# First stage of a two-layer decoder trunk: DMA order x, gate, x, up, and 256-column products for units 0 and 1

## The chip, the cores and the metric

The kernel runs on one core of one Trainium2 chip. The metric is the device time of one execution in microseconds (us), median of three runs. Besides these there is one profiled execution, from which all rows below come.

## The reference, cut to what matters

A trunk of two layers on a sequence of 256 tokens with 1024 channels, all float32. Each layer is SwiGLU, mixer, SwiGLU, each followed by a layer norm of `alpha*x + sub`; layer 0 mixes by causal pooling, layer 1 by sliding-window attention.

```python
def swiglu(x, w_gate, w_up, w_down):
    h = jax.nn.silu(x @ w_gate) * (x @ w_up)
    return h @ w_down
...
x = post_norm(x, 0.5 * swiglu(x, ffn_w_gate[i, 0], ...), ln_g[i, 0], ln_b[i, 0])
```

There are four SwiGLUs, each with gate and up matrices of 1024 x 2816 and a down matrix of 2816 x 1024. Only the first one's start is touched by the change.

## The kernel before, in words

The hidden width of 2816 is cut into 22 **units** of 128. For each unit TensorE (PE) makes gate and up products into PSUM (8 blocks of 128 input channels each), ScalarE (ACT) takes silu of the gate, VectorE (DVE) multiplies by up, and PE multiplies the result with the down weights into four accumulators (`ffn_down`). To reach float32 accuracy at speed, weights and activations are split into a high and a low part of type fp32r, and three fp32r products stand for one (`three`, L1056 to L1059). ACT makes the high part (L459 for gate and up, L467 for down), DVE the low part (L720, L724).

The first two units of every SwiGLU are not split: `gate_up_raw` (L1061) multiplies plain float32 weights `raw_g` with the channel-major activations `xf`, in two halves `t` of 128 tokens. The trace records each such float32 product as two matmuls, so that 8 channel blocks give 16 records. `xf` comes from `transposes(e, t)` (L1114, matmuls of L1123: 8 blocks of `xn`), whose first bank DVE copies (L797) and whose second ACT copies (L496). The order at the start of PE (L1132 to L1138), for the first SwiGLU, is: transposes of half 0; unit 0 half 0, gate and up; unit 1 half 0, gate; transposes of half 1; unit 1 half 0, up; unit 0 half 1; unit 1 half 1. Then come two small transposes of layer norm parameters (L1144), `ffn_down(0, 0)`, `gate_up(0, 2)` from split weights, `ffn_down(0, 1)` and so on.

The loads of the start are issued by SyncE's queue (SPq, L262 to L270) in this order: x half 0, gate unit 0, up unit 0, x half 1, gate unit 1, up unit 1 (512 KB each), down unit 0 (512 KB), gate and up of units 2 and 3 (1024 KB each), down unit 1 in two pieces, down units 2 and 3. The gate and up of unit 0 have semaphores of their own (`unit0_in[0]`, `unit0_in[1]`), those of unit 1 share `g_in[0]`, which has to reach 32. The load of units 4 and 5 overwrites the buffer of units 0 and 1 and waits for `g_used` = 2 (L238), which PE raises once per finished unit. Small loads, the identity matrix among them, are issued by ACT's queue.

ACT and DVE work through their instructions in program order: copies of both halves of `xf`, high and low parts of x (L510, L806), split of down unit 0, then per unit silu, high part of h, and for unit 0 also the split of unit 2's gate and up, then the split of the next down weights. `gate_up(0, 2)` waits for the low parts of unit 2 (`g_lo_done`, L1081).

Of the kernel before, what the change touches and what calls it, by code (L numbers as in the profile page):

```python
# [21 lines left out]
P = 128  # L22
D = 1024
S = 256
F = 2816
KT = D // P
TT = S // P
# [39 lines left out]
def trunk_kernel(nc, x, positions, ln_g, ln_b, w_gate, w_up, w_down, pool_w, pool_b, pool_scale,  # L67
# [8 lines left out]
    with ExitStack() as ctx:  # L76
# [21 lines left out]
        xf = sb("xf", [P, TT, KT, P])  # L98
# [28 lines left out]
        ps = ctx.enter_context(nc.psum_tensor("ps", [P, 8, 512], f32))  # L127
        ACC = [[ps[:, 2 * t + h, :] for h in range(2)] for t in range(TT)]
        WORK = 4

        g_in = [sem("g_in0"), sem("g_in1")]
        unit0_in = [sem("unit0_gate_in"), sem("unit0_up_in"), sem("unit0_down_in")]
# [69 lines left out]
        def raw_unit(G, half):  # L202

            c = raw_g[:, (G // 2) % 2, half, :].rearrange("p (k f) -> p k f", k=KT)
            return c[:, :, (G % 2) * P:(G % 2 + 1) * P]
# [18 lines left out]
        @block.sync  # L224
        def _(sp):
            gate_v = w_gate.rearrange("l i (k p) f -> (l i) p k f", p=P)
            up_v = w_up.rearrange("l i (k p) f -> (l i) p k f", p=P)
            down_v = w_down.rearrange("l i (u p) d -> (l i) p u d", p=P)
            qkv_v = w_qkv[0].rearrange("(k p) c -> p k c", p=P)
            wo_v = w_o[0].rearrange("(u p) d -> p u d", p=P)  # L230
            pool_v = pool_w[0].rearrange("g (k p) d -> p k g d", p=P)

            def load_gate_up(f, c, it=0):

                C = G0[f] // 2 + c

                if c == 2:
                    sp.wait_ge(g_used, G0[f] + RAW_UNITS)  # L238
                elif c > 2:
                    sp.wait_ge(g_lo_done, 2 * (X0[f] + 2 * c - 2) + 8 * it)  # L240
                elif f > 0:
                    sp.wait_ge(g_lo_done, 2 * (X0[f] + 2 * c))
                dst = raw_g[:, C % 2, :, :].rearrange("p m (k f) -> p m k f", k=KT)
                for m, w in enumerate((gate_v, up_v)):
                    sp.dma_start(dst[:, m], w[f, :, :, bass.ds(2 * P * c + 4 * P * it, 2 * P)]).then_inc(g_in[C % 2], 16)

            def load_down(f, c, it=0):

                E = D0[f] // 2 + c
                after(sp, d_lo_done, 2 * (E - 1) + 4 * it)  # L250
                for m in range(2):
                    sp.dma_start(raw_d[:, E % 2, m, :], down_v[f, :, bass.ds(2 * c + m + 4 * it, 1), :].rearrange("p a d -> p (a d)")).then_inc(d_in[E % 2], 16)

            def load_d(E, srcs):
                after(sp, d_lo_done, 2 * (E - 1))
                for m, src in enumerate(srcs):
                    dst = raw_d[:, E % 2, m, :]
                    sp.dma_start(dst.rearrange("p (g d) -> p g d", g=4) if len(src.shape) == 3 else dst, src).then_inc(d_in[E % 2], 16)


            first = raw_g[:, 0, :, :].rearrange("p m (k f) -> p m k f", k=KT)
            for t in range(TT):  # L262
                sp.dma_start(xn[:, t, :], x[0, t * P:(t + 1) * P, :]).then_inc(x_in[t], 16)
                for m, w in enumerate((gate_v, up_v)):
                    sp.dma_start(first[:, m, :, t * P:(t + 1) * P], w[0, :, :, t * P:(t + 1) * P]).then_inc(unit0_in[m] if t == 0 else g_in[0], 16)
            sp.dma_start(raw_d[:, 0, 0, :], down_v[0, :, 0, :]).then_inc(unit0_in[2], 16)
            load_gate_up(0, 1)
            for h in range(2):
                sp.dma_start(raw_d[:, 0, 1, 512 * h:512 * (h + 1)], down_v[0, :, 1, 512 * h:512 * (h + 1)]).then_inc(d_in[0], 16)
            load_down(0, 1)  # L270
            for f in range(FFNS):
                for c in range(2 if f == 0 else 0, 3):
                    load_gate_up(f, c)
                    load_down(f, c)
                with sp.Fori(0, (UNITS // 2 - 3) // 2) as it:
                    for c in range(3, 5):
                        load_gate_up(f, c, it)
                        load_down(f, c, it)
                if f == 0:
                    load_d(D_POOL // 2, [pool_v[:, k] for k in range(2)])  # L280
                if f == 2:

                    for i, j in enumerate((2, 0, 1)):
                        C = G_QKV // 2 + i
                        sp.wait_ge(g_lo_done, 2 * (X_QKV - 2 + 2 * i))
                        for m in range(2):
                            sp.dma_start(raw_g[:, C % 2, m, :].rearrange("p (k c) -> p k c", k=4),
                                         qkv_v[:, 4 * m:4 * m + 4, 512 * j:512 * (j + 1)]).then_inc(g_in[C % 2], 16)
                        if i < 2:
                            load_d(D_WO // 2 + i, [wo_v[:, 2 * i + m] for m in range(2)])  # L290
                    for i in range(2, 4):
                        load_d(D_WO // 2 + i, [wo_v[:, 2 * i + m] for m in range(2)])
            for t in range(TT):
                for h in range(2):
                    sp.wait_ge(y_done, 2 * t + h + 1)
                    sp.dma_start(out[0, t * P:(t + 1) * P, 512 * h:512 * (h + 1)], xn[:, t, 512 * h:512 * (h + 1)]).then_inc(out_done, 16)
            sp.wait_ge(out_done, 64)
# [755 lines left out]
        def _(pe):  # L1053
# [7 lines left out]
            def gate_up_raw(f, u, t, ms=(0, 1)):  # L1061

                e, G = FFN_EVENT[f], G0[f] + u
                if f > 0 and u == 0 and t == 0 or f == 0 and u == 1 and t == 0 and ms[0] == 0:
                    pe.wait_ge(g_in[(G // 2) % 2], 32 * (G // 4 + 1))
                for m in ms:
                    if f == 0 and u == 0 and t == 0:
                        pe.wait_ge(unit0_in[m], 16)

                    for i, k in enumerate((0, 4, 1, 5, 2, 6, 3, 7) if f > 0 else range(KT)):  # L1070
                        if m == 0 and u == 0:
                            pe.wait_ge((xf_lo_done, xf_up_done)[k // 4], 8 * e + 4 * t + k % 4 + 1)
                        last = pe.matmul(ps[:, WORK + u % 2, m * S + t * P:m * S + (t + 1) * P], raw_unit(G, m)[:, k, :],  # L1073
                                         xf[:, t, k, :], start=i == 0, stop=i == KT - 1)
                if t == TT - 1:
                    last.then_inc(g_used, 1)

            def gate_up(f, u, it=0):
# [50 lines left out]
            for f in range(FFNS):  # L1129
                e = FFN_EVENT[f]  # L1130

                transposes(e, 0, used=(0, 2, 1, 1)[f])  # L1132
                gate_up_raw(f, 0, 0)
                gate_up_raw(f, 1, 0, (0,))
                transposes(e, 1)
                gate_up_raw(f, 1, 0, (1,))
                gate_up_raw(f, 0, 1)
                gate_up_raw(f, 1, 1)  # L1138
                if f == 0:

                    pe.wait_ge(small_in, 64)
                    pe.wait_ge(xf_up_done, 8)
                    for a in range(2):
                        last = pe.transpose(ps[:, 7, 48 * a:48 * (a + 1)], lnrow[:, a, :], ident[0:48, 0:48])  # L1144
                    last.then_inc(lnT_ps, 1)
                ffn_down(f, 0)
                with pe.Fori(0, (UNITS - 6) // 4) as it:
                    for u in range(2, 6):
                        gate_up(f, u, it)
                        ffn_down(f, u - 1, it=it)  # L1150
                last_u = UNITS - 4
                gate_up(f, last_u)
                ffn_down(f, last_u - 1)
                gate_up(f, last_u + 1)
                ffn_down(f, last_u, (0,))
                gate_up(f, last_u + 2)
                ffn_down(f, last_u + 1, (0,))
                gate_up(f, last_u + 3)
                ffn_down(f, last_u + 2, (0,))
                ffn_down(f, last_u, (1,))  # L1160
                ffn_down(f, last_u + 3, (0,))
                ffn_down(f, last_u + 1, (1,))
                ffn_down(f, last_u + 2, (1,))
                if f != 2:
                    ffn_down(f, last_u + 3, (1,))
                if f == 0:
                    pool_pe(pe, three)
                if f == 2:
                    attention_pe(pe, three, down, transposes, lambda: ffn_down(2, UNITS - 1, (1,)))
# [39 lines left out]
```

## Time and profile before

| what | us |
|---|---|
| median of 3 runs | 919.07 |
| the three runs | 919.07, 917.87, 919.52 |
| span of the profiled execution, first to last instruction | 916.1 |
| PE busy in it | 875.6 (96%) |
| first raw float32 product starts | 7.09 |
| last raw float32 product of units 0 and 1 ended, parameter transposes start | 27.96 |
| last PE work of the span ends, about | 906 |

The page of the profile gives no device time for the profiled execution apart from its span; the median of the runs lies 2.97 us above the span. Times in rows are microseconds from the start of the span. A matmul's duration (275 ns and the like) contains its latency; successive matmuls overlap, so what counts for the time is the distance between their starts.

### The profile page before, as it was taken

The numbers are of one execution on the slowest core, as the hardware profiler recorded it, in microseconds if no ns is written. First come the engines' busy times: TensorE is split into PE (matmuls) and PEld (weight loads), VectorE is DVE, ScalarE is ACT, GpSimd is POOL, SyncE is SP. The second block draws the span as 40 slices with busy tenths as digits, with TensorE's granted clock in tenths as the row PEclk, the third lists the DMA queues.
The fourth block names the chain that finished last, engine by engine and source line by source line (L and its number), as shares of the span: only waits on it lengthen the run. The fifth ranks groups of instructions, "written<-read, shape, count | busy, mean of one in ns | idle before, by whom it ended". The sixth has DMA issues, their size and how long they took to land.

```text
span 916.1 us, 14933 instructions
## 1 busy us (share of the span) xinstructions
PE 875.6 (96%) x5954; PEld 805.0 (88%) x5954; DVE 540.4 (59%) x758; ACT 380.1 (41%) x622; POOL 76.3 (8%) x71
## 2 busy tenths in 40 slices
PE   6999999997999999999999999988999999999995
PEld 6999999986999999998999999976766899999994
DVE  1764455488674455447665545568687775445445
ACT  2444344322444344333434433435575434434430
POOL 0020000066100000001040000023000100000001
PEclk9999999999999999999999999999999999999998
DMA  9886546254485555660865565450127096555501
GB/s 293 304 289 219 183 160 207 97 176 141 170 301 184 197 172 181 211 202 2 275 239 184 173 217 175 161 218 15 42 101 254 20 311 234 183 189 177 184 1 46
DMA packets 116275, 162.30 MB, mean 177 GB/s; under 512 B 3968, under 2 KB 97760, under 8 KB 116240
## 3 DMA queue, kind: packets, MB, share of 16 engines
q1 hardware_dynamic: 112656, 152.06, 49.2%
q0 software_dynamic: 2496, 9.44, 2.8%
q8 instruction: 24, 0.39, 0.2%
q10 hardware_dynamic: 1088, 0.32, 0.1%
q14 instruction: 11, 0.09, 0.0%
HBM read 160.75 MB, written 1.05 MB: 177 GB/s over the span
## 4 chain that ended last, share of the span: by engine, by line
PE 82%; DVE 10%; ACT 3%; POOL 2%; issue 1%; DMA 1%; SPq 0%; POOLq 0%; DVEq 0%; ACTq 0%
PE ps L1057 25%; PE ps L1058 25%; PE ps L1059 25%; PE ps L1073 5%; DVE stats L759 2%; DVE xn L758 2%; DMA raw_g<-in_ffn_w_up 1%; POOL rstd L356 1%; DVE xn L774 1%; PE ps L1123 1%; PE ps L943 1%; ACT silu L403 1%; PE ps L934 1%; PE ps L937 1%; POOL rstd L358 1%
## 5 line engine op out<-in xcount | busy, mean ns | idle before, releaser
L1059 PE MATMUL ps<-xT_hi,g_lo 128*128 128x256 f32 x1280 | 362.2, 283 | 0.0
L1058 PE MATMUL ps<-xT_lo,g_hi 128*128 128x256 f32 x1280 | 362.2, 283 | 0.0
L1057 PE MATMUL ps<-xT_hi,g_hi 128*128 128x256 f32 x1280 | 361.8, 283 | 0.0
L1057 PEld LDWEIGHTS ps<-xT_hi,g_hi 128*128 128x128 f32 x1280 | 245.4, 192 | 3.2
L1058 PEld LDWEIGHTS ps<-xT_lo,g_hi 128*128 128x128 f32 x1280 | 245.4, 192 | 3.1
L1059 PEld LDWEIGHTS ps<-xT_hi,g_lo 128*128 128x128 f32 x1280 | 245.4, 192 | 0.0
L720 DVE TENSOR_TENSOR g_lo<-raw_g,g_hi 128x1024 fp32r<-128x1024 f32 x171 | 206.5, 1247 | 42.0 <-ACT g_hi L459 41.9
L471 ACT ACTIVATE silu<-ps 128x256 f32<-128x256 f32 x88 | 33.8, 384 | 393.0 <-PE ps L1059 386.1
L728 DVE TENSOR_TENSOR hf<-silu,ps 128x256 f32<-128x256 f32 x88 | 37.0, 421 | 263.0 <-ACT silu L471 263.0
L459 ACT ACTIVATE g_hi<-raw_g 128x1024 fp32r<-128x1024 f32 x172 | 172.0, 1052 | 4.9 <-PE ps L943 4.4
L1057 PE MATMUL ps<-d_hi,hT_hi 128*128 128x512 f32 x352 | 138.7, 394 | 2.0 <-DVE hT_lo L733 2.0
L1058 PE MATMUL ps<-d_lo,hT_hi 128*128 128x512 f32 x352 | 137.9, 392 | 0.0
L1059 PE MATMUL ps<-d_hi,hT_lo 128*128 128x512 f32 x352 | 137.0, 389 | 0.0
L724 DVE TENSOR_TENSOR d_lo<-raw_d,d_hi 128x1024 fp32r<-128x1024 f32 x98 | 122.8, 1254 | 2.6 <-ACT d_hi L467 2.6
L467 ACT ACTIVATE d_hi<-raw_d 128x1024 fp32r<-128x1024 f32 x98 | 102.7, 1049 | 3.1 <-PE ps L1059 3.0
L1059 PEld LDWEIGHTS ps<-d_hi,hT_lo 128*128 128x128 f32 x352 | 66.1, 188 | 14.5
L1057 PEld LDWEIGHTS ps<-d_hi,hT_hi 128*128 128x128 f32 x352 | 66.4, 189 | 14.0 <-DVE hT_lo L733 2.4
L1058 PEld LDWEIGHTS ps<-d_lo,hT_hi 128*128 128x128 f32 x352 | 66.4, 189 | 10.6
L1073 PE MATMUL ps<-xf,raw_g 128*128 128x128 f32 x512 | 61.7, 282 | 3.8 <-DMA raw_g<-in_ffn_w_up 3.2
L1073 PEld LDWEIGHTS ps<-xf,raw_g 128*128 128x128 f32 x512 | 60.1, 197 | 5.4 <-DMA raw_g<-in_ffn_w_up 3.4
L733 DVE TENSOR_TENSOR hT_lo<-hf,hT_hi 128x256 fp32r<-128x256 f32 x88 | 43.5, 494 | 5.3 <-ACT hT_hi L475 5.3
L475 ACT ACTIVATE hT_hi<-hf 128x256 fp32r<-128x256 f32 x88 | 35.9, 408 | 11.9 <-DVE hf L728 11.9
(137 smaller groups left out, 548.9 us busy)
## 6 DMA issues: line engine op xcount, KB each, us to landing
raw_d<-in_ffn_w_down SPq DMA_DIRECT2D x87, 512.0 KB, 4.0
raw_g<-in_ffn_w_gate SPq DMA_DIRECT2D x43, 1024.0 KB, 5.3
raw_g<-in_ffn_w_up SPq DMA_DIRECT2D x43, 1024.0 KB, 7.8
raw_g<-in_attn_w_qkv SPq DMA_DIRECT2D x6, 1024.0 KB, 6.6
raw_d<-in_attn_w_o SPq DMA_DIRECT2D x8, 512.0 KB, 3.7
gb<-in_ln_g POOLq DMA_DIRECT2D x6, 512.0 KB, 5.2
gb<-in_ln_b POOLq DMA_DIRECT2D x6, 512.0 KB, 6.3
xn<-in_x SPq DMA_DIRECT2D x2, 512.0 KB, 7.2
```

Of the source, the lines that this page charges most:

```text
L459: act.activation(g_half(g_hi, X, half), src(G, half), ACT.Copy).then_inc(g_hi_done, 1)
L467: act.activation(d_hi[:, E % D_SLOTS, :], raw_d[:, (E // 2) % 2, E % 2, :], ACT.Copy).then_inc(d_hi_done, 1)
L471: act.activation(silu[:, u % 2, :], ps[:, WORK + u % 2, 0:S], ACT.Silu).then_inc(silu_done, 1)
L475: act.activation(hT_hi[:, (D0[f] + u) % D_SLOTS, :], hf[:, u % 2, :], ACT.Copy).then_inc(h_hi_done, 1)
L720: dve.tensor_tensor(g_half(g_lo, X, half), src(G, half), g_half(g_hi, X, half).bitcast(f32), ALU.subtract).then_inc(g_lo_done, 1)
L724: dve.tensor_tensor(d_lo[:, E % D_SLOTS, :], raw_d[:, (E // 2) % 2, E % 2, :], d_hi[:, E % D_SLOTS, :].bitcast(f32), ALU.subtract).then_in ...
L728: dve.tensor_tensor(hf[:, u % 2, :], silu[:, u % 2, :], ps[:, WORK + u % 2, S:2 * S], ALU.mult).then_inc(hf_done, 1)
L733: dve.tensor_tensor(hT_lo[:, slot, :], hf[:, u % 2, :], hT_hi[:, slot, :].bitcast(f32), ALU.subtract).then_inc(h_lo_done, 1)
L1057: pe.matmul(out_, l_hi, r_hi, start=start, stop=False)
L1058: pe.matmul(out_, l_hi, r_lo, start=False, stop=False)
L1059: return pe.matmul(out_, l_lo, r_hi, start=False, stop=stop)
L1073: last = pe.matmul(ps[:, WORK + u % 2, m * S + t * P:m * S + (t + 1) * P], raw_unit(G, m)[:, k, :], xf[:, t, k, :], start=i == 0, stop=i = ...
```

## The change

The loads are issued as x half 0, gate unit 0, x half 1, up unit 0, gate unit 1, up unit 1. Everything behind them is as before. PE does unit 0's gate on half 0, transposes half 1, does unit 0's gate on half 1, and then unit 0's up, unit 1's gate and unit 1's up on all 256 tokens at once, each with one set of 8 float32 products (`gate_up_first`). The wait for unit 1's weights moves to the start of unit 1's gate. The other three SwiGLUs keep their order.

```diff
             for t in range(TT):
                 sp.dma_start(xn[:, t, :], x[0, t * P:(t + 1) * P, :]).then_inc(x_in[t], 16)
-                for m, w in enumerate((gate_v, up_v)):
-                    sp.dma_start(first[:, m, :, t * P:(t + 1) * P], w[0, :, :, t * P:(t + 1) * P]).then_inc(unit0_in[m] if t == 0 else g_in[0], 16)
+                sp.dma_start(first[:, t, :, 0:P], (gate_v, up_v)[t][0, :, :, 0:P]).then_inc(unit0_in[t], 16)
+            for m, w in enumerate((gate_v, up_v)):
+                sp.dma_start(first[:, m, :, P:2 * P], w[0, :, :, P:2 * P]).then_inc(g_in[0], 16)
...
-                if f > 0 and u == 0 and t == 0 or f == 0 and u == 1 and t == 0 and ms[0] == 0:
+                if f > 0 and u == 0 and t == 0:
                     pe.wait_ge(g_in[(G // 2) % 2], 32 * (G // 4 + 1))
...
-                if t == TT - 1:
+                if t == TT - 1 and ms[-1] == 1:
+                    last.then_inc(g_used, 1)
+
+            def gate_up_first(u, m):
+
+                if u == 0:
+                    pe.wait_ge(unit0_in[m], 16)
+                elif m == 0:
+                    pe.wait_ge(g_in[0], 32)
+                for k in range(KT):
+                    last = pe.matmul(ps[:, WORK + u % 2, m * S:(m + 1) * S], raw_unit(u, m)[:, k, :],
+                                     xf[:, :, k, :], start=k == 0, stop=k == KT - 1)
+                if m == 1:
                     last.then_inc(g_used, 1)
...
                 transposes(e, 0, used=(0, 2, 1, 1)[f])
-                gate_up_raw(f, 0, 0)
-                gate_up_raw(f, 1, 0, (0,))
-                transposes(e, 1)
-                gate_up_raw(f, 1, 0, (1,))
-                gate_up_raw(f, 0, 1)
-                gate_up_raw(f, 1, 1)
+                if f == 0:
+                    gate_up_raw(0, 0, 0, (0,))
+                    transposes(e, 1)
+                    gate_up_raw(0, 0, 1, (0,))
+                    gate_up_first(0, 1)
+                    gate_up_first(1, 0)
+                    gate_up_first(1, 1)
+                else:
+                    gate_up_raw(f, 0, 0)
+                    gate_up_raw(f, 1, 0, (0,))
+                    transposes(e, 1)
+                    gate_up_raw(f, 1, 0, (1,))
+                    gate_up_raw(f, 0, 1)
+                    gate_up_raw(f, 1, 1)
```

## Rows read from the trace of the kernel before

**Rows 1.** The page: busy time of each engine, share of the span.
```profile
PE 875.6 (96%) x5954; PEld 805.0 (88%) x5954; DVE 540.4 (59%) x758; ACT 380.1 (41%) x622; POOL 76.3 (8%) x71
```
**Rows 2.** Timeline of PE, 0 to 60 us (start, length, instruction, count, idle before).
```profile
5.03 1.97 PE L1123 MATMUL ps<-cst,xn 128*128 128x128 f32 x8 [5.03 <-DMA cst<-in_masks]
7.09 5.85 PE L1073 MATMUL ps<-xf,raw_g 128*128 128x128 f32 x32
16.17 2.05 PE L1073 MATMUL ps<-xf,raw_g 128*128 128x128 f32 x16 [3.22 <-DMA raw_g<-in_ffn_w_up]
18.06 1.04 PE L1123 MATMUL ps<-cst,xn 128*128 128x128 f32 x8
18.93 9.10 PE L1073 MATMUL ps<-xf,raw_g 128*128 128x128 f32 x80
27.96 0.32 PE L1144 MATMUL ps<-cst,ax 48*128 48x48 f32 x2
28.21 0.50 PE L1057 MATMUL ps<-d_hi,hT_hi 128*128 128x512 f32 x1
...
31.07 0.28 PE L1057 MATMUL ps<-xT_hi,g_hi 128*128 128x256 f32 x1
```
**Rows 3.** One line's instructions, L1073, 7 to 9 us: durations in ns.
```profile
L1073 PE MATMUL ps<-xf,raw_g x9: 421/421/550, 7.1 to 8.9; 128*128 128x128 f32 x9
```
**Rows 4.** One line's instructions, L894, whole span: durations in ns.
```profile
L894 PE MATMUL ps<-qT,xn x16: 275/331/421, 215.1 to 217.4; 128*128 128x128 f32 x16
```
**Rows 5.** Windows, PE only (busy, count, PEclk, DMA share, GB/s), 210 to 221 us.
```profile
217.00:218.00 1.00, 1.00 (x6) 0.50 0.00 0
```
**Rows 6.** Windows of 1 us (busy of PE, PEld, DVE, ACT, POOL; PEclk; DMA share; GB/s).
```profile
7.00:8.00 1.00, 0.91 (x4) 0.94 (x5) 0.00 (x0) 0.60 (x1) 0.00 (x0) 1.00 0.96 188
8.00:9.00 1.00, 1.00 (x7) 1.00 (x6) 0.00 (x0) 0.00 (x0) 0.00 (x0) 1.00 0.46 148
9.00:10.00 1.00, 1.00 (x7) 1.00 (x6) 0.00 (x0) 0.00 (x0) 0.00 (x0) 1.00 0.94 341
```
**Rows 7.** Timelines of PE in short windows, 10.9 to 11.6 us: records of up.
```profile
10.64 0.85 PE L1073 MATMUL ps<-xf,raw_g 128*128 128x128 f32 x3
...
11.06 0.77 PE L1073 MATMUL ps<-xf,raw_g 128*128 128x128 f32 x4
```
**Rows 8.** DMA issues of SPq in short windows: KB, us from issue to landing.
```profile
raw_g<-in_ffn_w_up SPq DMA_DIRECT2D x1, 512.0 KB, 7.1
xn<-in_x SPq DMA_DIRECT2D x1, 512.0 KB, 10.4
raw_g<-in_ffn_w_up SPq DMA_DIRECT2D x1, 512.0 KB, 11.0
raw_g<-in_ffn_w_up SPq DMA_DIRECT2D x1, 1024.0 KB, 10.5
```
**Rows 9.** Timeline of all engines, 0 to 60 us: issues of those four loads.
```profile
1.66 0.58 SPq L265 DMA_DIRECT2D raw_g<-in_ffn_w_up  x1
2.29 2.32 SPq L263 DMA_DIRECT2D xn<-in_x  x1
5.13 2.66 SPq L265 DMA_DIRECT2D raw_g<-in_ffn_w_up  x1
13.01 1.31 SPq L245 DMA_DIRECT2D raw_g<-in_ffn_w_up  x1
```
**Rows 10.** The same timeline: copies and splits by DVE and ACT.
```profile
6.25 0.69 DVE L797 COPY xf<-ps 128x512 f32<-128x512 f32 x1 [6.25 <-PE ps L1123]
18.76 0.69 DVE L797 COPY xf<-ps 128x512 f32<-128x512 f32 x1 [11.82 <-PE ps L1123]
25.68 1.99 ACT L459 ACTIVATE g_hi<-raw_g 128x1024 fp32r<-128x1024 f32 x2
26.76 2.36 DVE L720 TENSOR_TENSOR g_lo<-raw_g,g_hi 128x1024 fp32r<-128x1024 f32 x2 [0.52 <-ACT g_hi L459]
```
**Rows 11.** Timelines of PE, 647 to 660 and 205 to 215 us: float32 products, 256 columns.
```profile
652.13 1.89 PE L973 MATMUL ps<-kT,qT 128*128 128x256 f32 x8
...
207.38 3.69 PE L890 MATMUL ps<-qT,xn 128*128 128x256 f32 x16 [0.82 <-DVE xn L774]
```

## The prediction

> **What bounds the kernel now.** I read the page first: PE is busy for 96% of the span [rows 1], so the kernel ends when PE's row of work ends, and the change can bring or cost only what it does to PE between 0 and 31 us. Next the timeline of PE over that stretch [rows 2]. Transposes of half 0 start at 5.03, raw products at 7.09; 32 records (unit 0, half 0) end before 13, then PE stands still for 3.22 us until up of unit 1 lands at 16.17. From there it works without a gap: 16 records, 8 transposes, 80 records, parameter transposes at 27.96, down products at 28.21, unit 2 at 31.07. The only things to win are this gap, the slow first products and the price of 128 against 256 columns; behind 28 us the same work follows in the same order.
>
> The third view is the duration of single records. Those of 7 to 9 us take 421 ns [rows 3], against 275 ns as the shortest of the same form at [rows 4]. There 421 ns is the longest, and in 217 to 218 us the granted clock is 0.50 [rows 5], that is 1.2 GHz of 2.4. So PE starts at the lower level, although the clock column of 7 to 10 us says 1.00 [rows 6]; I go by the durations. The 16 records of unit 0's gate run from 7.09 to 10.64, where up begins [rows 7]: its third record starts at 11.06, (11.06 - 10.64)/2 = 0.21 us each. All 32 end at 12.94: from 11.28 the last 13 records follow at (12.67 - 11.28)/12 = 0.116 us, so the clock rises near 11.25, 4.2 us after the first product. At the higher level 80 records take 9.10 us, (9.10 - 0.275)/79 = 0.112 us each [rows 2].
>
> **The change, in PE's new order.**
> 1. Transposes of half 0 and unit 0's gate on half 0 are as before: 7.09 to 10.64.
> 2. Transposes of half 1 now stand at 10.64. They need x half 1. Before it was the fourth load, issued at 2.29 and landed 10.4 us later, at 12.69; the third, up of unit 0, issued at 1.66, landed after 7.1 us at 8.76 [rows 8, 9]. Equal in bytes, x half 1 as third load should land near 8.8; the bounds are 8.8 and 12.7, and I take 8.8, the row of the same place. So no wait. Three transposes at the lower level (0.21 each), five at the higher (18.06 to 18.93 is 0.87 for 8, 0.109 each): done at 11.8.
> 3. Half 1 of `xf` must be copied before the next product, and nothing of PE lies between now: a new wait. From first transpose to DVE's copy it was 1.22 us at the lower level (5.03 to 6.25) and 0.70 at the higher (18.06 to 18.76) [rows 2, 10]; mixed, I take 0.95. 10.64 + 0.95 + 0.69 copy + 0.15 to the product (6.94 to 7.09) = 12.43. PE idles about 0.6 us; before, half 0 of unit 1's up covered this copy. Behind this wait stand all later products, but no other engine.
> 4. Unit 0's gate, half 1: 16 x 0.112 = 1.79, to 14.2.
> 5. Unit 0's up, 16 records of 256 columns. Their distance is (1.89 - 0.379)/7 = 0.216 us in one row and (3.69 - 0.379)/15 = 0.221 in the other, taking 379 ns for the last record's own length [rows 11]. I take 0.217: 3.47, to 17.7. It needs the fourth load by 14.2; the old fourth landed at 12.69.
> 6. Unit 1, 32 x 0.217 = 6.94. It needs `g_in[0]` at 17.7; the sixth load landed at 5.13 + 11.0 = 16.1 [rows 8, 9], with the same bytes ahead of it. No wait. End: 24.6 to 24.7.
>
> Against 27.96 this is **3.3 us less**. By terms: the gap of 3.2 goes, 48 wide records instead of 96 narrow ones give 48 x (0.224 - 0.217) = 0.3, the copy wait takes 0.6, and more transposes but fewer products fall in the slow stretch, which with rounding gives the remaining 0.4. The width in itself is nearly worth nothing; it matters that no product of unit 1 stands before 17.7.
>
> **What is late next.** Down products at 24.9 need h of unit 0, finished some 7 us earlier than before because unit 0 ends at 17.7. Unit 2 would start at 31.07 - 3.3 = 27.8 and needs its low parts. Its up weights land at 13.01 + 10.5 = 23.5 [rows 8, 9], unchanged, since the bytes ahead are the same. From ACT's start to the end of DVE's second half it is 25.68 to 29.12, 3.44 us [rows 10], so 23.5 + 3.44 = 26.95: 0.8 us to spare, and a stall if that load is over 0.8 us later. This is the thinnest cover. ACT then splits down unit 1 and does silu of unit 1 about 2 us late, which has the 5.8 us of unit 2's products before `ffn_down(0, 1)`; the DVE work in between (1.2 + 2.4 + 0.4 us) ends near 31.4 against 33.5. The load of units 4 and 5 is released at 24.7 instead of 28.0, and moves with PE. SPq issues as many loads as before; ACT's and POOL's queues are passed by nothing. I cost all of this at nothing.
>
> **Sum.** The span becomes 916.1 - 3.3 = 912.8. The page has no device time of that execution; the median of the runs lies 2.97 above the span, so I carry the difference over: 919.07 - 3.3 = 915.8. A change of 0.2% is 1.84 us, about what a measurement of this kernel can tell from none; the three runs themselves spread over 1.65 us.
>
> **Rivals.**
> A. *Transfers come later where they are needed.* x half 1 at 12.69, as if its kind and not its place decided. Transposes then start at 12.7, 2.1 us late, all at the higher level, so that first product of half 1 starts at 12.7 + 0.70 + 0.69 + 0.15 = 14.2, 1.8 us later than above: a gain of 1.5, 917.6. For it: a poor rate of 188 and 148 GB/s at 7 to 9 us, where x half 1 was next in the queue [rows 6]. Against it: x half 0 landed before 5 us without harm. The same sum follows if up of unit 0 lands at 16 instead of before 14.2. Chance 0.15.
> B. *The clock rises later*, because transposes and the copy wait, not products, now stand at 10.64 to 12.4. If it is still low until 14.6, the 4 us of work from 10.64 runs at half speed: transposes to copy 1.22 and product at 12.70, 9 records by 14.6 instead of 19, end 1.2 to 1.4 us later: a gain of 2.0, 917.1. If it rises only at 16.1, sixteen records have taken 3.4 us from 12.70 and 48 x 0.217 remain: end 26.5, gain 1.4. For it: the rise came 4.2 us after products began, and they are now broken off after 3.55. Against it: transposes at 5.03 to 7 already preceded it. Chance 0.14 for both. The Trainium skill, "TensorE: Matmul & The Clock Gate", Part 4, says that transposes do not count as busy in the way that other matmuls do; by that rule the break in PE's activity would be 1.8 us long and B the likelier; no row here shows transposes alone at the moment of a rise.
> C. *Slower.* Changing 4 KB rows of x against 512-byte rows of weights ahead in the queue makes the whole first stream run at the dip's lowest rate, 148 GB/s [rows 6], instead of recovering to 341. Five loads of 0.524 MB behind x half 0 (landed about 4.7) then take 17.7 us: up of unit 1 lands at 22.4, unit 1 ends at 29.4, and units 2 and 3, late by the same 6.3 us, are split at 33.2 against a start of 31.07: 2.1 us slower, 921.2. It decides from where up of unit 1 lands after 21.0 (17.7 + 3.3), or units 2 and 3 after 27.6. Only a two-microsecond dip speaks for it. Chance 0.04.
> D. *It does nothing*, the gap merely reappearing before `gate_up(0, 2)` because the split of unit 2 ends at 30 or later, loads having been late by 3: 918 to 919. Chance 0.05.
> The forecast itself has the remaining 0.62.
>
> **How the numbers follow.** The forecast's own range is 915.8 with 0.5 for the copy wait and the time of the rise, and 0.8 for the spread of medians: 914.7 to 917.0. A and B add up to 918.0. Range 914.6 to 918.1, leaving out C, D and the edges. Faster by over 0.2% means below 917.2: nearly all of the forecast's 0.62, two thirds of B, a quarter of A and some of the small cases give 0.77; slower takes C, 0.04; the rest 0.19.
>
> **What would show it.** In the new profile: first raw product still at 7.1; transposes of half 1 at 10.6; a PE gap of 0.6 us before 12.4 released by DVE's copy and no wait on `raw_g`; 48 records of 256 columns 0.217 apart; parameter transposes at 24.6; unit 2 at 27.8. Transposes waiting for `xn` would be A; records of 421 ns or more behind 12.4 would be B; a gap before L1057 on `g_lo` would be D. The prediction is wrong if the parameter transposes start after 26, or if they start at 24.6 and the span does not fall by 3.

## The result, and the profile after

| | before | changed |
|---|---|---|
| median, us | 919.3 (4 runs, 917.87 to 920.16) | 914.65 (4 runs, 912.52 to 915.46) |
| profiled execution: time / span, us | 917.87 (worked out below) / 916.1 | 912.52 / 910.7 |

The ratio of the measurement is 0.9941, with a 95% interval of 0.9926 to 0.9956: 5.4 us faster, between 4.0 and 6.8. The two medians of four runs each lie 4.65 us apart, inside that interval; below, "by the ratio" and "by the medians" keep the two apart. The forecast was 3.3 us and 915.8 us. Its sign and the course of the first stage were right, its size was too small. Where both are on record, the device time of an execution lies 1.7 to 1.9 us above its span. So the profiled execution of before, with its span of 916.1, can only be the fastest of the first three, 917.87; this matters below. One execution of the kernel before, measured beside the first filled gap, took 1084.34 us at a mean granted clock of 0.751 and is left out of every comparison.

The timeline of PE in the changed kernel, first stage (start, length, instruction, count, idle before), answers to [rows 2]:

```profile
4.48 1.97 PE L1136 MATMUL ps<-cst,xn 128*128 128x128 f32 x8 [4.48 <-DMA cst<-in_masks]
6.55 3.67 PE L1074 MATMUL ps<-xf,raw_g 128*128 128x128 f32 x16
10.05 1.04 PE L1136 MATMUL ps<-cst,xn 128*128 128x128 f32 x8
11.51 2.05 PE L1074 MATMUL ps<-xf,raw_g 128*128 128x128 f32 x16 [0.42 <-DVE xf L798]
13.39 10.53 PE L1086 MATMUL ps<-xf,raw_g 128*128 128x256 f32 x48
23.85 0.32 PE L1165 MATMUL ps<-cst,ax 48*128 48x48 f32 x2
...
27.07 0.36 PE L1058 MATMUL ps<-xT_hi,g_hi 128*128 128x256 f32 x1
```

The order is the one forecast. No product waits for a load; the only gap shown inside the stage is that for DVE's copy, 0.42 us (forecast 0.6). The wide products stand (23.85 - 13.39)/48 = 0.218 us apart (forecast 0.217). The parameter transposes start at 23.85 instead of 27.96, 4.1 us earlier, and unit 2 at 27.07 instead of 31.07, 4.0 us.

The loads and the split of unit 2, from the views of DMA issues in short windows (us to landing), of SPq's issues, and of DVE, answer to [rows 8 to 10]:

```profile
raw_g<-in_ffn_w_gate SPq DMA_DIRECT2D x1, 512.0 KB, 5.0
xn<-in_x SPq DMA_DIRECT2D x1, 512.0 KB, 6.8
```
```profile
1.66 0.58 SPq L263 DMA_DIRECT2D xn<-in_x  x1
2.28 0.43 SPq L264 DMA_DIRECT2D raw_g<-in_ffn_w_up  x1
```
```profile
24.46 2.36 DVE L721 TENSOR_TENSOR g_lo<-raw_g,g_hi 128x1024 fp32r<-128x1024 f32 x2 [3.50 <-ACT g_hi L460]
```

x half 1 landed at 1.66 + 6.8 = 8.5, in time for 10.05. The low parts of unit 2 were ready at 26.82, and PE started it at 27.07, where its down products alone would have let it start near 26.96: the thin cover that the prediction named is used up.

Where did the rest of the two spans' difference go? The spans differ by 5.4 us, the first stage by 4.0. Starts of the same work later in the two executions, before first and changed second (timelines of PE, and one window of PE each: busy, count, PEclk, DMA share, GB/s):

```profile
207.38 3.69 PE L890 MATMUL ps<-qT,xn 128*128 128x256 f32 x16 [0.82 <-DVE xn L774]
419.59 1.11 PE L1123 MATMUL ps<-cst,xn 128*128 128x128 f32 x8 [0.72 <-DVE xn L774]
700.40 0.70 PE L981 MATMUL ps<-cst,hf 128*128 128x128 f32 x4 [1.89 <-DVE hf L647]
713.37 1.11 PE L1123 MATMUL ps<-cst,xn 128*128 128x128 f32 x8 [0.79 <-DVE xn L774]
```
```profile
702.00:703.00 1.00, 1.00 (x3) 0.50 0.30 91
```
```profile
203.45 3.69 PE L891 MATMUL ps<-qT,xn 128*128 128x256 f32 x16 [0.82 <-DVE xn L775]
415.65 1.11 PE L1136 MATMUL ps<-cst,xn 128*128 128x128 f32 x8 [0.72 <-DVE xn L775]
696.38 0.66 PE L982 MATMUL ps<-cst,hf 128*128 128x128 f32 x4 [1.88 <-DVE hf L648]
708.04 1.11 PE L1136 MATMUL ps<-cst,xn 128*128 128x128 f32 x8 [0.79 <-DVE xn L775]
```
```profile
698.00:699.00 1.00, 0.96 (x4) 1.00 0.28 89
```

The lead is 3.93, 3.94 and 4.02 us up to 700 us and 5.33 at 713. Between them the granted clock of the execution of before was 0.50 for over three microseconds; in that of the changed kernel it was not. Nothing in this stretch was edited. That the two spans also differ by 5.4 us, the gain of the runs, is a coincidence: 4.0 in the first stage and 1.3 here. So the profile gives 4.0 us to the first stage, the runs give 5.4, and the experiments had to find the difference.

### The profile page after: what moved, and what is told of

It is laid out like the page before. It is cut to its first block, busy times and chain, and to the rows that moved or that the text cites. A ratio compares the mean times of both kernels' runs of the same rounds, so it can differ in the third digit from the quotient of the medians.

```text
span 910.7 us, 14837 instructions
## 1 busy us (share of the span) xinstructions
PE 873.6 (96%) x5906; PEld 801.9 (88%) x5906; DVE 539.2 (59%) x758; ACT 380.4 (42%) x622; POOL 76.2 (8%) x71
## 4 chain that ended last, share of the span: by engine, by line
PE 83%; DVE 10%; ACT 3%; POOL 2%; issue 1%; DMA 0%; POOLq 0%; DVEq 0%; ACTq 0%
PE ps L1058 25%; PE ps L1059 25%; PE ps L1060 25%; PE ps L1074 4%; DVE stats L760 2%; DVE xn L759 2%; PE ps L1086 1%; POOL rstd L357 1%; DVE xn L775 1%; PE ps L1136 1%; PE ps L944 1%; ACT silu L404 1%; PE ps L935 1%; PE ps L938 1%; DVE hT_lo L734 1%
## 5 line engine op out<-in xcount | busy, mean ns | idle before, releaser
L1074 PE MATMUL ps<-xf,raw_g 128*128 128x128 f32 x416 | 50.4, 283 | 0.9 <-DVE xf L798 0.4
L1074 PEld LDWEIGHTS ps<-xf,raw_g 128*128 128x128 f32 x416 | 48.9, 197 | 2.6 <-issue 1.1
```

## The experiments

Three theories. **G**: the old gap of PE costs more than its length, because in many executions the clock is at 1.2 GHz behind it, and the change takes that away too. **R**: the surplus comes from clock stretches of later stages, by chance. **B**: after the change the load and split of unit 2 is the next bound, so that more speed in front of it brings nothing. Medians are compared with the kernel before on the same chip.

**The kernel before, unaltered, in a second profile.**

> The kernel before once more, for a second profile. Theory S (the earlier first transpose of the changed kernel, 4.48 instead of 5.03 us, comes from the order of the loads): first transpose again near 5.0, parameter transposes near 28.0. Rival V (it varies from run to run): first transpose anywhere from 4.4 to 5.1. Theory P (the second stretch at the lower clock, at 700 us, is a matter of where the rise and fall fall in an execution): the number of low stretches before 900 us may be one or two, and the span then 914.5 or 916 us.

Timeline of PE and, below it, windows of PE (busy, count, PEclk, DMA share, GB/s):

```profile
4.79 1.97 PE L1123 MATMUL ps<-cst,xn 128*128 128x128 f32 x8 [4.79 <-DMA cst<-in_masks]
6.85 5.52 PE L1073 MATMUL ps<-xf,raw_g 128*128 128x128 f32 x32
16.76 3.64 PE L1073 MATMUL ps<-xf,raw_g 128*128 128x128 f32 x16 [4.39 <-DMA raw_g<-in_ffn_w_up]
20.24 1.04 PE L1123 MATMUL ps<-cst,xn 128*128 128x128 f32 x8
21.11 9.10 PE L1073 MATMUL ps<-xf,raw_g 128*128 128x128 f32 x80
...
30.14 0.32 PE L1144 MATMUL ps<-cst,ax 48*128 48x48 f32 x2
```
```profile
16.00:17.00 1.00, 0.24 (x1) 0.85 1.07 374
17.00:18.00 1.00, 1.00 (x6) 0.50 1.09 371
18.00:19.00 1.00, 1.00 (x6) 0.50 1.10 354
19.00:20.00 1.00, 1.00 (x7) 0.50 1.11 352
20.00:21.00 1.00, 1.00 (x10) 0.94 1.09 344
```

The span was 918.2 us. The gap is 4.39 us, and behind it the clock goes to 0.50 until about 20: the same 16 records take 3.64 instead of 2.05 us. From their start to the parameter transposes it is 13.38 us here and 11.79 in [rows 2], 1.6 more, and the load landed 0.6 later. The profile on which the prediction rests had escaped this. The other 18 runs on that chip spread from 917.70 to 922.06, 4.4 us against 1.65 in the three runs of the prediction. The first transpose came at 4.79, which neither confirms nor excludes S. I had expected parameter transposes near 28.0 and a span of 914.5 or 916: both were missed, because the fall behind the gap was in none of the theories. The stretch near 700 us was there again (0.50 from 702 to 706).

**The changed kernel, unaltered, twice.**

> The changed kernel once more, in more rounds. If 4.0 us come from the first stage and the other 1.3 us of the two profiles from the clock's stretches at 700 us, which differ from run to run, the median difference from before lies at 4.0 to 4.7 us (ratio 0.995 to 0.9956), not at 5.4. If the 5.4 us are all of the change, the ratio is again 0.994.

> The changed kernel unaltered, beside the next two on one chip: median near 914.3, 5.5 to 6 us below the kernel before. If the surplus over the 3.6 us of the first stage is the lower clock behind the old gap, the profile again shows no stretch at 0.5 before 205 us.

Medians 914.21 against 920.14 (ratio 0.9938, 0.9921 to 0.9956) and 914.81 against 919.54 (0.9956, 0.9943 to 0.9969). That is 5.9 and 4.7 us by the medians, 5.7 and 4.0 by the ratios. The first expectation, 4.0 to 4.7, was missed the first time and met at its edge the second; the other expectation, 5.5 to 6, was missed. In both profiles no stretch at 0.50 stands before 205 us, the parameter transposes start at 23.82 and 23.73, and unit 2 starts at 26.93 and 26.96. Stretches at 0.50 in later stages do vary: none between 215 and 900 us in the first, one at 610 in the other. The first transposes start at 4.59 and 4.93, against 4.48 above for the same kernel: this start varies from run to run.

**Only the loads reordered.**

```diff
-                for m, w in enumerate((gate_v, up_v)):
-                    sp.dma_start(first[:, m, :, t * P:(t + 1) * P], ...)
+                sp.dma_start(first[:, t, :, 0:P], (gate_v, up_v)[t][0, :, :, 0:P]).then_inc(unit0_in[t], 16)
+            for m, w in enumerate((gate_v, up_v)):
+                sp.dma_start(first[:, m, :, P:2 * P], ...).then_inc(g_in[0], 16)
```

> New order of loads, old order of products. Theory S: first transpose at 4.5 us. The gap before the load of unit 1's up at 16.1 us decides in any case, so products of unit 1 start at 16 and parameter transposes at 27.9 to 28.1: same time as before (0 to -0.3 us); a second, new wait of some 1.9 us for unit 0's up (landing 12.5) shows inside the first gap. Rival: the loads alone bring half of the gain (-2 us).

Timeline of PE:

```profile
6.66 3.43 PE L1074 MATMUL ps<-xf,raw_g 128*128 128x128 f32 x16
12.16 3.02 PE L1074 MATMUL ps<-xf,raw_g 128*128 128x128 f32 x16 [2.07 <-DMA raw_g<-in_ffn_w_up]
16.06 3.78 PE L1074 MATMUL ps<-xf,raw_g 128*128 128x128 f32 x16 [0.87 <-DMA raw_g<-in_ffn_w_up]
...
29.65 0.32 PE L1145 MATMUL ps<-cst,ax 48*128 48x48 f32 x2
```

Ratio 0.9988 (0.9978 to 0.9999), 919.27 us against 920.14: about 1 us less, where I had expected 0 to 0.3 and the rival 2. The wait is only divided (2.07 and 0.87 us), and the clock fell here too (0.50 from 13 to 19 us, when PE had been back at work for some 0.8 us), so that the parameter transposes came at 29.65, not at 28 as I had written.

**Only the products reordered**, with the loads as before.

```diff
...
+                if f == 0:
+                    gate_up_raw(0, 0, 0, (0,))
+                    transposes(e, 1)
+                    gate_up_raw(0, 0, 1, (0,))
+                    gate_up_first(0, 1)
+                    gate_up_first(1, 0)
+                    gate_up_first(1, 1)
...
```

> New order of products, old order of loads. x half 1 lands at 12.7, so PE waits 2 us before the transposes of half 1; then 0.70 + 0.69 + 0.15 to the product at 14.2, and 1.8 + 10.45 us of products: parameter transposes at 26.5, 1.5 us less than before. Rival (the order of the products is all of it): 4 us less as with both. Theory S: first transpose at 5.0 us.

```profile
6.83 2.78 PE L1073 MATMUL ps<-xf,raw_g 128*128 128x128 f32 x16
13.52 1.97 PE L1135 MATMUL ps<-cst,xn 128*128 128x128 f32 x8 [3.91 <-DMA xn<-in_x]
15.49 3.55 PE L1073 MATMUL ps<-xf,raw_g 128*128 128x128 f32 x16
18.88 10.53 PE L1085 MATMUL ps<-xf,raw_g 128*128 128x256 f32 x48
29.34 0.33 PE L1164 MATMUL ps<-cst,ax 48*128 48x48 f32 x2
```

Ratio 0.9972 (0.996 to 0.9985), 917.58 us, 2.6 less where I had expected 1.5. PE waits 3.91 us for x half 1, and the clock is at 0.50 from 12 to 18 us: transposes take 1.97 and the next 16 records 3.55. So the parameter transposes came at 29.34, not at 26.5, 0.8 us before those of the kernel before in its second profile; the two spans differ by 2.0 us, and the other 1.2 came later, where the stretch at 0.50 stood at 616 instead of 702. Neither part alone brings half of the 5.9 us by which the changed kernel leads on the same chip (0.9 and 2.6 by the medians); the products must be reordered so that unit 1 stands last, and x must come earlier so that this order has its data.

**The gap filled in the kernel before**, with products whose result is left out; run twice.

```diff
                 gate_up_raw(f, 0, 0)
+                if f == 0:
+                    for i in range(13):
+                        pe.matmul(ACC[0][0][:, 0:P], raw_unit(0, 0)[:, i % KT, :], xf[:, 0, i % KT, :], start=True, stop=True)
                 gate_up_raw(f, 1, 0, (0,))
```

> The kernel before, with 13 extra float32 products of 128 columns (26 records, 2.9 us) into a free accumulator bank in PE's gap before unit 1; they are left out of the result, since the bank is started afresh later. Theory G (in many executions the wait of 3 to 4 us for up of unit 1 also brings the clock down to 1.2 GHz behind it, 2 us more, and the change removes both): PE is never idle for long, the clock stays high behind the gap, nothing else changes: median 1 to 2 us below the kernel before, none of its runs above 919.5. Rival R (the spread between 917.7 and 922 comes from later stages): same median as before. Rival L (the order of transfers alone sets the gain): same as before.

> The kernel before with its gap filled by extra products, once more, since the first interval only just excluded no change. Theory G: no stretch at 0.5 before 205 us in this second profile either, parameter transposes at 27.5 to 28.0, no run above 919.5, median 1 to 2 us below the kernel before. Rival R: a median within 0.5 us of the kernel before and runs up to 921.5.

Timeline of PE in the first of the two:

```profile
6.74 5.88 PE L1073 MATMUL ps<-xf,raw_g 128*128 128x128 f32 x32
12.45 3.07 PE L1136 MATMUL ps<-xf,raw_g 128*128 128x128 f32 x26
15.78 2.05 PE L1073 MATMUL ps<-xf,raw_g 128*128 128x128 f32 x16 [0.26 <-DMA raw_g<-in_ffn_w_up]
...
27.57 0.32 PE L1147 MATMUL ps<-cst,ax 48*128 48x48 f32 x2
```

More work for PE, and a faster kernel: 918.78 against 919.86 (ratio 0.9985, 0.9974 to 0.9997), and 917.67 against 919.55 (0.9983, 0.9974 to 0.9992). That is 1.4 and 1.6 us less by the ratios, 1.1 and 1.9 by the medians. No run of the 23 is above 919.29, while the kernel before reached 921.7 beside the first of the two and 920.66 beside the second. In both profiles the 16 records behind the gap take 2.05 us, and no stretch at 0.50 stands before 205. In the second the load was late (products of unit 1 at 16.32, after 1.03 us of waiting), so that the parameter transposes came at 28.11, just outside the 27.5 to 28.0 expected. The time until the load lands is still there; what is gone is the low clock behind it.

The mean granted clock, which every run has and not only the profiled ones, says the same. It is 0.9900 on average over 61 runs of the kernel before (nine of them at 0.987), 0.9916 over the 23 with the gap filled (none below 0.989), and 0.9919 over 14 of the changed kernel. One stretch of 3.4 us at 0.50 costs 1.7 us of clock, 0.0019 of the span. An estimate from these figures: the filled gap takes away 0.0016, 1.5 us, and the changed kernel 0.0019, 1.7 us. So filling the gap alone raises the clock nearly as much as the whole change does. G holds, and R, as the main source of the surplus, falls. What is left for R is the difference of 0.0003, some 0.3 us; by the scatter of the runs it is uncertain by about 0.5 us, and the runs come from several chips.

**The changed kernel with narrow products.**

```diff
-                for k in range(KT):
-                    last = pe.matmul(ps[:, WORK + u % 2, m * S:(m + 1) * S], raw_unit(u, m)[:, k, :],
-                                     xf[:, :, k, :], start=k == 0, stop=k == KT - 1)
+                for t in range(TT):
+                    for k in range(KT):
+                        last = pe.matmul(ps[:, WORK + u % 2, m * S + t * P:m * S + (t + 1) * P], raw_unit(u, m)[:, k, :],
+                                         xf[:, t, k, :], start=k == 0, stop=k == KT - 1)
```

> The changed kernel with unit 0's up and unit 1 in two halves of 128 columns each (96 records instead of 48). 96 x 0.112 = 10.75 us against 10.46: parameter transposes 0.3 us later, at 24.1; time 0 to 0.5 us above the changed kernel (914.5). Rival W (the width is the gain): back up by 2 us or more.

```profile
13.38 10.88 PE L1087 MATMUL ps<-xf,raw_g 128*128 128x128 f32 x96
24.19 0.32 PE L1166 MATMUL ps<-cst,ax 48*128 48x48 f32 x2
```

The 96 narrow records take 10.81 us to the parameter transposes, the 48 wide ones 10.46: 0.35 us. The median of 913.39 (ratio 0.9936) does not show it: it is at the changed kernel's ratios of 0.9938 and 0.9941. The changed kernel did not run beside this one or the next two, so they are compared by their ratios to the kernel before. The width is not the gain; the order is.

**The transposes moved in, and the mask load deferred.** In the first of two kernels the copy of `xf` is covered by the last four records of unit 0's first gate; in the second the 192 KB of attention masks are loaded later as well.

```diff
-                    gate_up_raw(0, 0, 0, (0,))
+                    gate_up_raw(0, 0, 0, (0,), range(0, 6))
                     transposes(e, 1)
+                    gate_up_raw(0, 0, 0, (0,), range(6, 8))
```
```diff
-            act.dma_start(cst[:, 1:4, :], masks[1:4].rearrange("m p q -> p m q")).then_inc(cst_in, 16)
...
             gp.wait_ge(g_used, 4)
+            gp.dma_start(cst[:, 1:4, :], masks[1:4].rearrange("m p q -> p m q")).then_inc(cst_in, 16)
```

> The changed kernel with the transposes of half 1 put between blocks 0 to 5 and 6 to 7 of unit 0's first gate, so that four records cover DVE's copy. The idle 0.41 us goes: parameter transposes at 23.4 to 23.5. But unit 2's low parts are done at 26.8 in the changed kernel's profile because its up load lands at 23.3, so theory B (the load of unit 2 is the next bound) expects unit 2 to start at 26.9 to 27.1 as now, with a new PE gap of 0.3 us before it, and the time within 0.2 us of the changed kernel. Rival: 0.4 us faster.

> As the kernel with the transposes moved in, and the 192 KB load of the attention masks, which ACT's queue issues at 3.5 us, moved to POOL's queue behind unit 3. Theory B: 0.2 MB less ahead of unit 2's up, some 0.5 us at 350 GB/s, so it lands at 22.8, its low parts are done at 26.3 and unit 2 starts at 26.5 to 26.6: 0.4 to 0.5 us faster than the changed kernel. Rival (PE is the bound anyway): no difference from the kernel with the transposes alone.

DVE's split of unit 2 in the one, then in the other:

```profile
24.31 2.36 DVE L721 TENSOR_TENSOR g_lo<-raw_g,g_hi 128x1024 fp32r<-128x1024 f32 x2 [3.44 <-ACT g_hi L460]
```
```profile
23.34 2.36 DVE L721 TENSOR_TENSOR g_lo<-raw_g,g_hi 128x1024 fp32r<-128x1024 f32 x2 [3.58 <-ACT g_hi L461]
```

In the first the gap of 0.41 is gone, the parameter transposes start at 23.60 and unit 2 at 26.92, just behind the split that ends at 26.67; 914.31 us (ratio 0.9945). In the second the split ends at 25.70, 1.0 earlier, more than the 0.5 expected, but PE itself was later in that execution (transposes from 4.75, parameters at 23.77), so unit 2 starts at 26.89, not at 26.5 to 26.6; 913.56 us (ratio 0.9936). Both ratios are within the changed kernel's three (0.9938 to 0.9956) or just beside them; of B they show only that the two bounds stand within some 0.3 us of each other.

**PE kept busy before its first data**, alone, and together with all the above and a wait for the gate half alone in front of unit 2. The extra products' results are left out.

```diff
+            dve.memset(hf[:, 0, 0:P], 0.0).then_inc(warm_in, 1)
...
+            pe.wait_ge(warm_in, 1)
+            for i in range(8):
+                pe.matmul(ACC[0][0][:, 0:P], hf[:, 0, 0:P], hf[:, 0, 0:P], start=True, stop=True)
             pe.wait_ge(ident_in, 16)
```
```diff
-                pe.wait_ge(g_lo_done, 2 * X + 2 + 8 * it)
+                first2 = f == 0 and u == RAW_UNITS
+                pe.wait_ge(g_lo_done, 2 * X + (1 if first2 else 2) + 8 * it)
...
                 for m in range(2):
+                    if first2 and m == 1:
+                        pe.wait_ge(g_lo_done, 2 * X + 2 + 8 * it)
```

> The changed kernel with 8 extra products of a zeroed tile (16 records, about 3.4 us) on PE before the identity matrix lands; their result is left out. If activity alone brings the clock up, it is high from about 5 us on, the first 16 records take 1.8 instead of 3.5 us, and PE then runs into its loads: transposes of half 1 wait for x until 8.5, up of unit 0 until 12.5, unit 1 ends at 23.0 instead of 23.8. Theory B (the load and split of unit 2 is the next bound): unit 2 still starts at 26.8 and the time is within 0.3 us of the changed kernel. Rival (PE's slow start is worth its 1.7 us): 1.7 us faster. Theory Z (zero data or the wait after it leaves the clock low): first records at 421 ns as before.

> The same extra products, with the transposes of half 1 moved in, the mask load deferred, and unit 2's gate products waiting for the low part of the gate alone. The split of unit 2 starts about 22.3 and its gate half is done at 24.6, so PE's own row decides again: unit 1 ends at 23.0, unit 2 starts at 26.1, 0.8 to 1.0 us before the changed kernel's: median near 913.3.

Timeline of PE, the extra products alone:

```profile
1.06 3.39 PE L1145 MATMUL ps<-hf 128*128 128x128 f32 x16 [1.06 <-DVE hf L819]
4.68 1.09 PE L1138 MATMUL ps<-cst,xn 128*128 128x128 f32 x8 [0.23 <-DMA cst<-in_masks]
6.28 2.02 PE L1076 MATMUL ps<-xf,raw_g 128*128 128x128 f32 x16 [0.51 <-DMA raw_g<-in_ffn_w_gate]
...
12.58 3.72 PE L1088 MATMUL ps<-xf,raw_g 128*128 128x256 f32 x16 [0.90 <-DMA raw_g<-in_ffn_w_up]
16.48 7.17 PE L1088 MATMUL ps<-xf,raw_g 128*128 128x256 f32 x32 [0.18 <-DMA raw_g<-in_ffn_w_up]
23.58 0.32 PE L1170 MATMUL ps<-cst,ax 48*128 48x48 f32 x2
...
27.36 0.36 PE L1060 MATMUL ps<-xT_hi,g_hi 128*128 128x256 f32 x1 [0.49 <-DVE g_lo L722]
```

The clock is up when the transposes begin: they take 1.09 us and the 16 records 2.02, where the changed kernel needs 3.11 to 3.67. All of it is given back to loads (0.90 and 0.18 us) and to the split of unit 2 (0.49): unit 2 starts at 27.36, no sooner. That is B, in this profile. The median, though, is 913.52 against 914.81 for the changed kernel on the same chip (ratios to before 0.9931 and 0.9956), 1.3 less where I had expected at most 0.3. The profiled execution was among its slower ones (912.3 of 909.5 to 912.9 in span), and where the others gained has no profile. The mean clock of the six runs is 0.992, that of the changed kernel's five 0.9916, which can explain some 0.4 us of it. So B holds for the one execution that was profiled and is not shown for the kernel: this stays open.

With everything together PE starts unit 2 at 25.45, since without the mask load unit 1's weights are there by 15.2 and unit 2's by 22.4:

```profile
11.68 10.74 PE L1088 MATMUL ps<-xf,raw_g 128*128 128x256 f32 x48
22.35 0.32 PE L1174 MATMUL ps<-cst,ax 48*128 48x48 f32 x2
25.45 0.28 PE L1060 MATMUL ps<-xT_hi,g_hi 128*128 128x256 f32 x1
```

911.88 us, ratio 0.9917 (0.9904 to 0.993), 7.7 us below the kernel before and 2.9 below the changed one: more than the 1.5 us expected, faster than both kernels. Which of its four parts brings how much is not separated.

## Why the prediction was right in kind and too small

**Steps 1 and 2** held in form. x half 1, as third load, landed at 8.5 for a forecast of 8.8, and rival A did not come. But PE was earlier: the parameter transposes came at 23.85, 23.82 and 23.73 in three profiles, forecast 24.6. The first transpose is not the reason: it began at 4.48, 4.59 and 4.93, and the transposes of half 1 followed at 10.05, 10.02 and 9.94 all the same. The reason is the rise of the clock, which I had put at 11.25 from one execution, the latest of all the profiles without early extra products: here all transposes of half 1 ran at the higher level (1.04 us for 8). This gives 0.6 us up to the transposes and 0.3 in them and the copy, of which 0.1 is lost again behind: 0.8 in all.

**Steps 3 to 6** held: copy gap 0.42 for 0.6, wide distance 0.218 for 0.217, unit 1 without a wait, the sixth load at 4.58 + 11.5 = 16.1 as in before. The width was worth 0.35 us (0.3 in the sum). What is late next was also named rightly: 26.82 for the split of unit 2 against a forecast of 26.95. That PE came to this 0.8 us sooner than forecast used the cover up. (The forecast's own range is slightly off: 915.8 with 0.5 and 0.8 on either side is 914.5 to 917.1, not 914.7 to 917.0.)

**The step that failed is the term "the gap of 3.2 goes".** I priced the gap at its length, in an execution in which the clock stayed up behind it. Of four profiles with a gap of this kind (the two of the kernel before, only the loads, only the products) the clock went to 0.50 in three. In the kernel before that costs 1.6 us more behind the gap. Filling the gap alone gives 1.4 and 1.6 us by the ratios, without any change of order. The 4.0 us of the first stage in the profile and these 1.5 make 5.5, against 5.4 (4.0 to 6.8) measured; the agreement to 0.1 is luck, since the two repetitions gave 5.7 and 4.0. So the sum fell 0.7 us short of the profiled execution's first stage, by the rise of the clock (steps 1 and 2), and a further 1.5 short of the median, by this term: with the 1.8 us between a time and its span, the profiled execution was the fastest run of three, while I carried the difference over to the middle one as if the two had the same clock. The spread of the runs (1.65 us in the first three, 4.4 in the 18), which I had read as noise, was partly the very cost that the change removes: in 61 runs of the kernel before the spans are 915.9 to 916.2 where the mean clock is 0.992, and 919.4 to 920.3 where it is 0.987.

**Rival B** had the right subject and the wrong direction: I asked whether the new order would bring the clock up later, not whether the old gap brought it down. The rule of the Trainium skill ("TensorE: Matmul & The Clock Gate", Part 4) that made B the likelier did not decide: in three profiles the clock was up when the transposes of half 1 began, so none of them shows what transposes alone do. Part 1 of the same page of the Trainium skill says that the point of the transition varies from run to run; the runs here agree, since the same 16 first records took 3.67, 3.53 and 3.11 us in three executions of one kernel. **Rivals C and D** did not come: up of unit 1 landed at 16.1 as before, up of unit 2 at 23.3 against 23.5. (Up of unit 0, now fourth, landed at 12.5, 0.9 us before PE needed it at 13.39.)

The 1.3 us between the two profiles at 700 us cannot be put down to the change. A stretch at 0.50 between 610 and 707 us stands in one of three profiles of the changed kernel, and in all eleven others: both of the kernel before, both with the filled gap, and seven further variants, five of which end the first stage earlier than the changed kernel or at most 0.5 us later. Whether the change itself makes that stretch rarer is not settled by three profiles; by the mean clocks of the runs it would be worth some 0.3 us, uncertain by 0.5.

## What to carry to other kernels

A gap of two to four microseconds on TensorE had two prices here: its length, and the lower clock that may follow it. Read the second from several executions, since a single profile may have escaped it; runs that are slower the lower their mean granted clock are the sign. Before pricing a sum against a median, ask which run was profiled and what its mean granted clock was. When the order is improved, ask what load comes due next: here, 0.4 to 1.7 us saved on PE in front of unit 2 were given back in the profiles until the loads themselves were thinned out, though the median of one of these kernels fell by 1.3 all the same.

## What the runs showed of the hardware

- Extra products in a gap made the kernel 1.4 to 1.6 us faster by the ratios, though they do nothing for the result.
- The granted clock went to 0.50 in three of four executions with a gap of PE of 2.07 to 4.39 us in the first stage, and in none of the ten whose gaps, behind the wait for the first data, were 1.03 us or less. The length alone does not decide: a wait of 2.07 us was followed by a fall, one of 3.22 us was not.
- The fall can come within the gap (at 11.9 us of a wait that lasted from 9.6 to 13.5) or when PE is back at work (at 13.0, with products again from 12.16).
- Products of a zeroed tile also bring the clock up: after 16 records from 1.06 us, the transposes at 4.68 ran at the higher level; in the other kernel with the same products they took 1.88 us from 4.63, at the lower, and the records behind them ran at the higher.
- The landing of the 64 KB identity matrix, issued at 0.74 us, let PE begin at 4.48 to 4.93 us in seven profiles with the new order of loads and at 4.67 to 5.03 in five with the old: the two ranges overlap, so the order of the loads does not set it.
